# Two held weight splits moved behind the norm columns in a two-layer backbone kernel

## The reference, cut to what matters

```python
def half_step_ffn(x, g_pre, g_post, shift, scale, gate, w_gate, w_up, w_down):
    h = modulated_norm(x, g_pre, shift, scale)          # rms_norm(x, g) * (1 + scale) + shift
    y = (jax.nn.silu(h @ w_gate) * (h @ w_up)) @ w_down # D_FF = 2816
    return x + FFN_RES * gate * rms_norm(y, g_post)

m_lat = (jax.nn.silu(c) @ w_mod[i] + b_mod[i])          # 9 rows: shift, scale, gate of 3 sub-layers
x = half_step_ffn(x, ...)
h_lat = modulated_norm(x, g[2], m_lat[:, 3], m_lat[:, 4])
y_lat = mixer_ab(h_lat, h_ctx, ...)   # layer 0: attention and short convolution
y_lat = hyena_mixer(h_lat, ...)       # layer 1: h @ w_in (3072 columns), long convolution, @ w_out
x = x + m_lat[:, 5] * rms_norm(y_lat, g[3])
x = half_step_ffn(x, ...)
```

## The kernel before, in words

| seam | norms | from, to | us in the trace |
|---|---|---|---|
| A | 6, 7 | output projection of layer 0, FFN stage 1 | 626 to 646 |
| B | 8, 9 | FFN stage 1, FFN stage 2 | 837 to 857 |
| C | 10, 11 | FFN stage 2, hyena input projection | 1055 to 1075 |
| D | 12, 13 | hyena output projection, FFN stage 3 | 1213 to 1233 |

## Time and profile before

### The profile page before, as it was taken

One profiled execution on the slowest core, in us unless ns is written; L12 is line 12 of the kernel. 1 busy time (PEld: TensorE's weight loads), 2 busy tenths in 40 slices (PEclk: granted clock), 3 DMA queues, 4 the chain that ended last, 5 costly groups with the idle time before them and its releaser, 6 DMA issues.

```text
span 1425.5 us, 21722 instructions
## 1 busy us (share of the span) xinstructions
PE 1362.0 (96%) x7850; PEld 1133.8 (80%) x7850; DVE 954.6 (67%) x1393; ACT 609.0 (43%) x924; POOL 129.8 (9%) x213
## 2 busy tenths in 40 slices
PE   6999999999899999999999999999999998899997
PEld 2578777877678976578888988889877876889996
DVE  1488876887766843558787668786775685775554
ACT  2433232333356543455444464443454332644443
POOL 2100110111101302211111001100000021000000
PEclk9999999999999999999999999999999999999999
DMA  9464557677746643138888748865533442556662
GB/s 332 164 207 148 202 197 264 229 255 266 254 138 187 175 136 89 15 129 320 278 299 277 230 137 294 283 236 191 163 112 110 133 133 98 209 196 189 185 186 74
DMA packets 76359, 275.11 MB, mean 193 GB/s; under 512 B 9226, under 2 KB 9781, under 8 KB 75712
## 3 DMA queue, kind: packets, MB, share of 16 engines
q1 hardware_dynamic: 52128, 187.00, 39.5%
q0 software_dynamic: 24160, 87.12, 18.6%
HBM read 273.04 MB, written 1.05 MB: 192 GB/s over the span
## 4 chain that ended last, share of the span: by engine, by line
PE 68%; DVE 14%; DMA 7%; ACT 5%; issue 5%; DVEq 0%; ACTq 0%; SPq 0%; POOL 0%; POOLq 0%
PE gu L1394 13%; PE gu L1396 13%; PE gu L1395 13%; DMA raw<-in_wstream_dram 6%; PE acc L1455 6%; PE acc L1456 6%; PE acc L1457 6%; DVE wlo L835 6%; ACT whi L509 3%; DVE part L852 3%; PE acc L1444 2%; PE gu L1536 1%; DVE act L1008 1%; PE acc L1825 1%; PE acc L1715 1%
## 5 line engine op out<-in xcount | busy, mean ns | idle before, releaser
L835 DVE TENSOR_TENSOR wlo<-raw,whi 128x1024 fp32r<-128x1024 f32 x350 | 428.9, 1235 | 210.5 <-ACT whi L509 209.1
L1394 PE MATMUL gu<-h_hi,whi 128*128 128x256 f32 (+1 forms) x1776 | 550.5, 310 | 9.3 <-DVE h_lo L950 6.2
L1395 PE MATMUL gu<-h_lo,whi 128*128 128x256 f32 (+1 forms) x1776 | 542.8, 306 | 0.0
L1396 PE MATMUL gu<-h_hi,wlo 128*128 128x256 f32 (+1 forms) x1776 | 542.6, 305 | 0.0
L509 ACT ACTIVATE whi<-raw 128x1024 fp32r<-128x1024 f32 x350 | 365.5, 1053 | 188.1 <-DMA raw<-in_wstream_dram 74.5
L1394 PEld LDWEIGHTS gu<-h_hi,whi 128*128 128x128 f32 x1776 | 335.9, 189 | 40.2 <-issue 14.6
L1395 PEld LDWEIGHTS gu<-h_lo,whi 128*128 128x128 f32 x1776 | 336.3, 189 | 20.3 <-issue 2.9
L1396 PEld LDWEIGHTS gu<-h_hi,wlo 128*128 128x128 f32 x1776 | 336.3, 189 | 16.7
L852 DVE SCALAR_TENSOR_TENSOR part<-wm,cvec,part 128x512 f32<-128x512 f32 x266 | 199.6, 750 | 6.5
L1455 PE MATMUL acc<-whi,act_hi 128*128 128x512 f32 x440 | 177.7, 404 | 13.9 <-DVE act_lo L1013 8.7
L1456 PE MATMUL acc<-whi,act_lo 128*128 128x512 f32 x440 | 175.0, 398 | 0.0
(11 more groups left out here) (210 smaller groups left out, 1080.3 us busy)
## 6 DMA issues: line engine op xcount, KB each, us to landing
raw<-in_wstream_dram SPq DMA_DIRECT2D x350, 512.0 KB, 4.3
wm<-in_wmod_dram POOLq DMA_DIRECT2D x136, 512.0 KB, 5.4
area<-in_wmod_dram POOLq DMA_DIRECT2D x8, 512.0 KB, 6.8
z<-in_gate_rows_dram POOLq DMA_DIRECT2D x6, 512.0 KB, 6.0
gate_keep<-in_gate_rows_dram POOLq DMA_DIRECT2D x5, 512.0 KB, 6.1
area<-in_rpb_dram POOLq DMA_DIRECT2D x32, 64.0 KB, 3.3
x_lat<-in_x_in_dram SPq DMA_DIRECT2D x1, 1024.0 KB, 8.1
area<-in_ctx_in_dram SPq DMA_DIRECT2D x1, 1024.0 KB, 11.4
```

The source lines that it names most:

```text
L835: nc.vector.tensor_tensor(wlo[:, u.base % RING, :], raw[:, u.base % RAW, :], whi[:, u.base % RING, :].bitcast(F32), ALU.subtract).then_inc ...
L1394: nc.tensor.matmul(out_, w_hi, x_hi, start=start, stop=False, skip_group_check=True)
L1395: nc.tensor.matmul(out_, w_hi, x_lo, start=False, stop=False, skip_group_check=True)
L1396: return nc.tensor.matmul(out_, w_lo, x_hi, start=False, stop=stop, skip_group_check=True)
```

## The change

On ACT, `norms` splits u4 and u5 after `h_his(q + 1)`; before, u4 came after `square(q, 1)` and u5 between `square(q + 1, 0)` and `square(q + 1, 1)`. On DVE, `norms` splits both after `h_los(q + 1)`; before, between the second `spread` and `h_los`. In C the hand-written ACT queue is changed likewise, and in addition the three `spectrum_out` now all stand ahead of `square(11, 0)`. PE, SP and POOL keep their order. The lines of the changed kernel are numbered up to 3 lower.

```diff
@@ ACT norms(q, held)
                 square(q, 0)
                 square(q, 1)
-                for u in held[:1]:
-                    split(Unit(u))
                 if q + 1 < len(NORMS):
                     square(q + 1, 0)
-                    for u in held[1:]:
-                        split(Unit(u))
                     square(q + 1, 1)
                     h_his(q + 1)
+                for u in held:
+                    split(Unit(u))
@@ ACT, seam C
             square(10, 0)
             square(10, 1)
-            split(Unit(U_HY + 4))
-            spectrum_out(0)
+            for i in range(3):
+                spectrum_out(i)
             square(11, 0)
-            split(Unit(U_HY + 5))
             square(11, 1)
-            spectrum_out(1)
-            spectrum_out(2)
             h_his(11)
+            for u in (U_HY + 4, U_HY + 5):
+                split(Unit(u))
@@ DVE norms(q, held)
                 post(q)
                 spread(q + 1, 0)
                 spread(q + 1, 1)
+                h_los(q + 1)
                 for u in held:
                     split(Unit(u))
-                h_los(q + 1)
```

## The result

The changed kernel takes 1434.07 us, the median of five runs (1431.22 to 1439.28); the kernel before, beside it, 1426.71 us (1425.72 to 1427.23). The ratio is 1.0057 with a 95% interval from 1.0034 to 1.0081: slower, by about 8 us. The forecast was 1432.3 us. The record holds 38 executions of the changed kernel in all, with a median of 1434.67 us; the kernel before, timed again beside the experiments, has medians of 1424.63 to 1425.47 us. That second comparison, +9 to +10 us, mixes chips.

A forecast was written before the change was run, and what follows sets the result against it. In turns with jobs the weight ring (load, `whi`, `wlo`, load) was taken as the bound. A +1.5, B +0.5, C +2.5 and D +1.5 made +6.0 us, so a median of 1432.3 us, range 1427.5 to 1437.

The forecast's parts named there:

- Part 1: Splits moved out of the way of the first `h_lo`: 0 us at A and D, B's start -0.78 us.
- Part 2, ACT's order: First turn after A, B, D: two `whi` ahead of the table load delay `whi` of u6, +0.85 us (B +0.15).
- Part 2, loads: Late `wlo` sends loads of u7 and u8 into POOL's burst; with ACT's delay, +1.5 at A and D, +0.5 at B.
- A's term: Seam A and its first turn: +1.5 us, taken between +0.85 and +1.95.
- the stage's term: Stage behind seam B: late loads partly covered by a start 0.78 us earlier; B as a whole +0.5 (bounds +0.15 and +1.2).
- D's: Seam D and its first turn: +1.5 us, as at A.
- Rival 3: Starved loads: u8 needs 8 to 10.8 us beside POOL's burst, A, B, D +3 to +5 each, 1438 to 1440; chance 0.10.
- Part 3: Seam C: third copy delays the squares, PE idles 2.56 us, clock falls to 0.50; +2.5 us (+0.9 to +3.95).
- The sum: All four seams: A +1.5, B +0.5, C +2.5, D +1.5 make +6.0 us, median 1432.3 us.
- Rival 2: `h_lo` waits for the removed splits at all four seams, -3.1 us, stream loses nothing, about 1423; chance 0.08.
- Rival 1: Small loss, +2.75, about 1429.1: u7 and u8 land in time and the clock at C stays up; chance 0.20.

The follow-up runs named there:

- dve_late_abd: Kernel before with only DVE's two splits late at A, B and D, ACT keeping its early splits: 1433.94 us, ratio 1.0059.
- after_gates_late: Changed kernel with POOL's gate and gain loads of stages 1 and 2 behind the first four `wm` pieces, D left: 1433.92 us, ratio 1.0050.
- c_spectra_first_warm: Kernel before with the three spectrum copies ahead of the squares at C, plus 11 unread identity products on PE before the columns: ratio 1.0007.
- norms_only: Changed kernel with seam C left as before, so the late splits at A, B and D alone: 1431.75 us, ratio 1.0042.
- c_spectra_first: Kernel before with only ACT's three spectrum copies ahead of both squares at C, splits left early: 1427.22 us, ratio 1.0002.
- the late gates: Kernel before with POOL's gate and gain loads of A and B behind the first turn's four `wm` pieces: 1429.65 us, ratio 1.0038.

## Why the prediction was right

The direction, the places and the mechanism were right, and the time fell inside the range. The loads' terms were less than half of what the rows show, so that the total came out right is in part luck, as the sum below tells. The terms, one by one:

**Part 1.** Right to 0.1 us. PE starts 640.36 - 638.43 = 1.93 us behind L562 at A, as before, and A is 13.94 us in both. B became 0.72 us shorter, for 0.78 predicted, and by the two steps named: the columns run without the gap, and PE waits for `h_lo` 1.15 us instead of 1.67. At A and D the splits that stood beside PE's columns had cost nothing, since those columns ran at the lower clock; the exception, with the clock up, is in the last section.

**Part 2, ACT's order.** `whi` of u6 follows the table load at 646.81, 647.1 in the sum. This +0.85, which I had as the lower bound, is real in the rows but decides nothing: dve_late_abd, which doesn't have it, is as slow.

**Part 2, loads.** The mechanism was right and its term too small. I had u8 land near 652.1; it landed at 655.34. The step that failed is the drain of the burst, 2.62 MB at 340 to 405 GB/s. Three things were missing from it. First, the engines were not full: from 646 to 650 us they moved 236 and 283 GB/s (us, then busy by engine, PEclk, DMA share, GB/s),

```profile
646.00:648.00 2.00, 2.00 (x19) 2.00 (x18) 1.97 (x4) 1.99 (x4) 0.00 (x0) 1.00 0.79 236
648.00:650.00 2.00, 2.00 (x19) 2.00 (x18) 2.00 (x4) 0.55 (x2) 0.53 (x1) 1.00 0.80 283
```

where in before the same two windows are full:

```profile
646.00:648.00 2.00, 2.00 (x19) 2.00 (x18) 0.66 (x1) 1.33 (x2) 0.53 (x1) 1.00 1.06 442
648.00:650.00 2.00, 2.00 (x19) 2.00 (x18) 2.00 (x5) 1.06 (x2) 0.00 (x0) 1.00 0.96 391
```

Second, POOL's `wm` piece was no longer in the burst's front but behind DVE's moved splits, at 648.84 instead of 646.18, so it ran into the loads of u7 and u8 (the next one, at 651.80, too). Third, at A alone, POOL's filter tables were still draining when the burst began. In after_gates_late, where POOL issues nothing between 638 and 648 us, its queue still moved 0.61 MB from 644 to 646 us:

```profile
q0 software_dynamic: 90, 0.61, 72.0%
```

At my own two rates that is 1.5 to 1.8 of the 3.2 us by which u8 landed late. On the second point I had written that POOL keeps its order and only its wait for `h_lo` moves; I had not looked at its wait for `part`. The late loads and the late piece are DVE's queue again: what is put at its end delays not only SP's loads but POOL's.

In size: A's term was +1.5. `wlo` of u8, where I had placed the delay, came 4.2 us later behind A's start, and the next turn gave nothing back, as I had written. The two traces show +6.5 for the whole stage; over all executions stage 1 has a mean of 195.66 with the early splits (six) and 199.77 with the late ones (197.82, 197.92 and 203.56), +4.1. At B the stage's term was +1.28 (+0.5 and the 0.78 that the start gives); the pair shows +1.68, the means 206.68 (four, both splits late) against 203.80 (four), +2.9. D's was +1.5: the pair shows +1.37, the means 190.85 (four) against 188.30 (eight), +2.5. So the three stages come to +9.5 by the means, where I had 4.3. Rival 3 had +3 to +5 for each on the condition that u8 lands 8 to 10.8 us after its issue; at A it landed after 8.33.

**Part 3.** Right in the pair: 2.56 us of idle predicted and 2.57 measured, L562 4.69 us behind the first column as predicted, clock 0.50, the seam +2.40 for +2.5. Two corrections. Before's own execution had the slower of two forms of C: 18.73 us with the granted clock at 0.50 from 1071 to 1074 us, behind the columns, where it keeps 1.00 in the faster form, which takes 17.8. So against the faster form the change costs 3.3, and against the mean of the five, 18.2, it costs 3.0. The share of the clock is less sure. I had put +0.9 for the case that the clock stays, so 1.6 us for its fall, and A and D with late splits show 1.63 us for it. In c_spectra_first_warm only 0.28 us came back, but there the early splits of ACT and DVE hold the columns and `h_lo` back, which is not the changed kernel's case. The rest, +0.8 to +1.7, is then the late squares, an estimate too.

**The sum.** By the means the terms are A +4.1, B 2.9 - 0.7 = +2.2, C +3.0 and D +2.5, together 11.8; the medians differ by 7.4, and the interval of the ratio is +4.9 to +11.6. norms_only shows the same gap: +3.1 to +8.8 by its time, 8.8 by the means. The forecast of +6.0 therefore stands nearer to the time than to its own terms, and this is luck: had the time followed the terms, it would have been about 1438.5 us, above the range. Against the 38 executions of the changed kernel, +9 to +10, the gap is smaller. C's part is seen in traces alone: c_spectra_first is no slower clear of noise, and dve_late_abd without C is as slow as the full change. That the terms overshoot the time is not explained: each rests on three to eight single executions whose stages scatter by 2 to 6 us.

**Rivals.** Rival 2, that the splits are what `h_lo` waits for, is refuted where the clock falls: A is 13.94 us with and without. Where it stays up its condition holds in part (the last section), but the loads take more than it gives. Rival 1 falls with the waits of u7 and u8. Rival 3 was nearer to the truth at A than its chance of 0.10 said.

## What to carry to other kernels

Work that stands in front of the critical instruction of a seam may cost nothing, if the engine would idle there for another one: read the idle right behind it before moving it. And a cheap instruction that frees a buffer is worth its place in the queue not by its own length but by the transfer it releases: ask which loads will go out at its new time and what else is in the DMA engines then. A burst that is moved away from one place falls on the next one, as the late gates did, so look for a stretch with a free rate before moving it. And a profile is one execution: with stages that scatter by 2 to 6 us, a size read from one pair of profiles needs several more executions or a launch time beside it.

## What was not expected of the hardware

**A load can get almost nothing beside loads of the other queue, even when the engines have room.** From 646.5 to 649 us of the changed kernel, with the load of u7 issued at 645.88 and that of u8 at 647.01 (DMA view: packets, MB, share of 16 engines):

```profile
q0 software_dynamic: 185, 0.68, 86.8%
q1 hardware_dynamic: 2, 0.01, 0.8%
```

The start of a load explains little of this: in after_gates_late the same load is issued at 645.57 and its first packets move between 646.4 and 646.6 us. From 649 to 653 us it turns round, and SP's queue has 65.0%. Then it is POOL's turn to wait: from 650.5 to 652.5 us its queue has 7.7% and SP's 92.4%, although POOL's `wm` piece was issued at 648.84. The Trainium skill ("DMA: Bandwidth & Descriptors", section "Queues, rings and completion order") has each engine take turns between queues packet by packet; 2 packets against 185 is no such turn, and the trace speaks against it for this stretch. Only behind it, from 653 to 655.5 us, do the shares come out even, 50.2% and 52.7%. From 646.5 to 653 us it looks as if the loads were served in the order of their issue, whichever queue they are on, and the 100.3% of POOL's queue with u9's load due fits this too. But it is no rule: in the kernel before, from 639 to 644 us, POOL's filter tables have 167 packets and the loads of u7 and u8 156, which is turn by turn. What decides between the two is open; no run tried it.

**The same idle does not always lower the clock.** At D, PE idles 2.38 to 2.40 us before the columns in each of the twelve traces. In the profiled execution of before they take 5.47 us, in that of dve_late_abd 3.84 (PE's timeline, then a window in it):

```profile
1225.19 3.84 PE L1448 MATMUL acc<-diag,x_lat 128*128 128x128 f32 x32 [2.39 <-DVE diag L933]
```

```profile
1225.50:1226.00 0.50, 0.50 (x7) 0.50 (x6) 0.00 (x0) 0.47 (x3) 0.00 (x0) 1.00 0.00 0
```

The granted clock reads 1.00 here and 0.50 in before's. With the splits late D is then 12.31 us (A too, in dve_late_abd) instead of 12.7: once the clock stays up, DVE's two splits are in the way by 0.4 us, as rival 2 had it. Over all executions D has 12.3 or 12.7 in six and 13.8 to 14.0 in six, so a difference of 1.3 us in one seam is no effect of an edit unless it repeats.
